# Prompt attention scores of a hybrid decoder step: from zero-padded keys, head by head, to 64-partition keys, heads in pairs

## The chip, the cores and the metric

The kernel runs on one core of a Trainium2 chip. The metric is the device time of one execution in microseconds (us). All data and all matmuls are float32. Five engines work beside each other: TensorE (PE, with its weight loads listed apart as PEld), VectorE (DVE), ScalarE (ACT), GpSimd (POOL) and SyncE (SP), which issues the transfers.

## The reference, cut to what matters

One layer takes 512 prompt tokens and 8 sequences of 4 new tokens over a paged cache. It has latent attention (MLA, 8 heads) and sparse attention (NSA, 8 heads in 2 groups of 4, each group with its own keys and values of 64 numbers). The change lies in NSA for the prompt. It has three branches; with 8 selected blocks at most, the selected branch sees all earlier tokens of a 512-token prompt, as the window branch does:

```python
s = einsum('btghd,bngd->bghtn', q, k_compressed) * 64**-0.5     # branch 1: 32 compressed blocks
p = masked_softmax(s, cmp_end[None, :] <= q_pos[:, None])
...
s = einsum('btghd,bkgd->bghtk', q_rot, k_sel_or_win) * 64**-0.5 # branches 2 and 3: rotated queries, causal
o = einsum('bghtk,bkgd->btghd', masked_softmax(s, causal), v)
out = gate0 * o_cmp + gate1 * o_sel + gate2 * o_win             # then * silu(z), one output projection, LayerNorm
```

## The kernel before, in words

`plan()` writes one list of steps by hand, and every engine walks this same list and issues its part of each step in that order; semaphores hold an engine back until what it needs is there. Stages follow each other: input projections and the compression of the caches (0 to about 290 us of the profile), then a stage in which the decode attention of the 8 sequences and the prompt's NSA are woven together (290 to 526), then the prompt's MLA with the output projections (526 to 675).

The prompt's attention is cut into units `UNITS`: a tile i of 128 queries, a branch (`pcmp`, `psel`, `pwin`, `pmla`) and a head h (for `pcmp` a group). NSA has 4 x (2 + 8 + 8) = 72 units, and `psel` and `pwin` 64 of them. A unit is a line of work over four engines: `scores` on TensorE into one of two PSUM banks (pool S); on VectorE a scaled and masked copy into a slot of `Pp` with the row minimum (`min_unit`), which frees the bank; on ScalarE the exponential (`exp_unit`); on TensorE i+1 transposes (`turn_p`) into one of two banks of pool T; a copy to `PTp` by ScalarE for even units and VectorE for odd ones; and on TensorE i+1 products with the values (`values`). `slot(m)` puts the scores of unit m, the transposes of unit m - `T_LAG` and the values of unit m - `V_LAG` into one step of the plan. `weave` then mixes the 72 slots with the decode steps by their weights, so that decode steps fill the gaps between slots. Pool T serves the decode steps too (transposes of key pages and of probabilities).

The queries of the two groups lie in the two halves of the partitions: `qrT` holds, for each hh, head hh of group 0 in partitions 0 to 63 and head hh of group 1 in 64 to 127. The keys `selKT` and `winKT` lie in the same way. Scores of one head are taken over all 128 partitions: GpSimd has made `padK` in the buffer `mid`, in which each group's keys stand in their half and the other half is zero (the steps `pad`). The compressed branch (`pcmp`) takes its scores over 64 partitions already, four small matmuls per group. A matmul of the program is two in the trace, each with its weight load, since its float32 weights are taken in two pieces; a transpose is one.

The lines that the steps below speak of: 828 and 833 projections, 803 every transpose (`turn`), 968, 969 and 971 scores of the decode items, 1021 their values, 1034 compressed scores, 1050 scores of `psel` and `pwin`, 1044 of `pmla`, 1081 values, 1669 and 1675 the masked copies, 1392 the exponentials, 1471 and 1817 the copies to `PTp`, 1911 and 1915 the padded keys.

## Time and profile before

| what | value |
|---|---|
| median of 3 runs | 674.38 us (672.66 to 680.26) |
| span of the profiled execution (from its first to its last instruction; no time of its own beside the span is recorded) | 675.0 us |
| busy: PE, DVE, ACT, POOL | 609.6, 286.9, 214.3, 93.7 us |
| mean granted clock of TensorE, 1 being 2.4 GHz | 0.960 |

Busy time is the union of an engine's instructions; matmuls are pipelined, so that a matmul's listed duration is longer than the distance to the next one's start. In this text the cost of a piece of TensorE's work is the distance between starts. A name such as `64*128` in a TensorE row is the size of the piece of the array that the instruction uses, rows by columns.

### The profile page before, as it was taken

The page shows a single profiled execution, that of the slowest core. Times are in us where ns is not written, and L with a number is a line of the kernel's source. Part 1 is how long each engine was busy: PE and PEld are TensorE (multiplying, and loading weights), DVE is VectorE, ACT ScalarE, POOL GpSimd, SP SyncE. Part 2 cuts the span into 40 slices and gives each one's busy share as a digit, 9 for nine tenths or more (in the row PEclk, how much of TensorE's full clock was granted, in tenths as well). Part 3 has the DMA queues.
Part 4 walks back from the last instruction along what each step waited for, and adds up shares of the span by engine and source line. Part 5 has one row for each costly group of instructions (what it writes and reads, how often), then busy time and mean ns, then how long its engine had stood idle before and what let it go on. Part 6 is the DMA issues. An engine that isn't in the chain of part 4 may idle for free. (4 is left out here: it accounts for less than half of the span.)

```text
span 675.0 us, 10193 instructions
## 1 busy us (share of the span) xinstructions
PE 609.6 (90%) x3482; PEld 375.2 (56%) x3482; DVE 286.9 (43%) x758; ACT 214.3 (32%) x614; POOL 93.7 (14%) x175
## 2 busy tenths in 40 slices
PE   6889998978897999879999899999999898999995
PEld 3554554555566865554446366666566765465642
DVE  0122202263658455653345334445444345255335
ACT  1330102241324221242343243445245345053310
POOL 0114531110100320420010001021003121000000
PEclk9889997989897989959999989999999998999999
DMA  8916563368407512223302105032401701010101
GB/s 307 263 47 144 106 155 51 47 87 118 100 1 236 212 26 74 74 74 110 109 18 70 57 1 188 1 111 79 125 2 62 289 2 40 1 62 1 63 0 62
DMA packets 42381, 60.34 MB, mean 89 GB/s; under 512 B 8986, under 2 KB 34074, under 8 KB 41722
## 3 DMA queue, kind: packets, MB, share of 16 engines
q1 hardware_dynamic: 42330, 59.69, 32.3%
q8 instruction: 28, 0.46, 0.3%
q14 instruction: 23, 0.19, 0.1%
HBM read 55.43 MB, written 8.41 MB: 95 GB/s over the span
## 5 line engine op out<-in xcount | busy, mean ns | idle before, releaser
L828 PE MATMUL psum<-wring,bufA 128*128 128x512 f32 (+2 forms) x384 | 159.2, 570 | 2.0 <-DMA wring<-in_w_in 2.0
L828 PEld LDWEIGHTS psum<-wring,bufA 128*128 128x128 f32 x384 | 74.9, 200 | 72.8 <-issue 67.4
L1392 ACT ACTIVATE wring<-wring,small 128x128 f32<-128x128 f32 (+3 forms) x96 | 53.9, 561 | 160.4 <-DVE small L1675 160.0
L1675 DVE CUSTOM_DVE_ANT_0 wring<-psum,const 128x128 f32<-128x128 f32 (+3 forms) x96 | 46.6, 486 | 86.5 <-PE psum L1050 75.1
L803 PE MATMUL psum<-const,ring 128*128 128x128 f32 (+2 forms) x360 | 52.2, 281 | 24.7 <-ACT mid L590 11.8
L803 PEld LDWEIGHTS psum<-const,ring 128*128 128x128 f32 (+2 forms) x360 | 37.9, 138 | 38.6 <-ACT mid L590 13.7
L1278 PE MATMUL psum<-ring,comp 128*128 128x512 f32 x128 | 56.5, 595 | 1.5 <-issue 1.5
L803 PE MATMUL psum<-const,wring 128*128 128x128 f32 x272 | 49.6, 280 | 6.8 <-ACT wring L1471 3.9
L803 PEld LDWEIGHTS psum<-const,wring 128*128 128x128 f32 x272 | 34.2, 143 | 33.6 <-issue 18.5
L1050 PE MATMUL psum<-mid,qrT 128*128 128x128 f32 (+3 forms) x128 | 50.1, 475 | 2.2 <-DVE small L1669 2.2
L1081 PE MATMUL psum<-kv,wring 128*128 128x64 f32 x320 | 43.8, 268 | 1.0 <-DVE rtmp L1703 0.8
L590 DVE COPY mid<-psum 64x256 f32<-64x256 f32 (+1 forms) x80 | 30.5, 381 | 32.6 <-PE psum L803 31.7
L1081 PEld LDWEIGHTS psum<-kv,wring 128*128 128x128 f32 x320 | 41.7, 195 | 3.0 <-DVE rtmp L1703 1.9
L1278 PEld LDWEIGHTS psum<-ring,comp 128*128 128x128 f32 x128 | 23.8, 190 | 29.0 <-issue 29.0
L891 PE MATMUL psum<-mid,w1h 128*128 128x256 f32 (+1 forms) x160 | 33.8, 366 | 0.0
L1954 POOL TENSOR_TENSOR bufA<-bufA,rtmp 128x512 f32<-128x512 f32 x8 | 10.2, 1271 | 151.4 <-DVE rtmp L1703 151.4
L891 PEld LDWEIGHTS psum<-mid,w1h 128*128 128x128 f32 x160 | 28.5, 197 | 4.1 <-issue 1.0
L590 ACT COPY mid<-psum 64x256 f32<-64x256 f32 (+1 forms) x80 | 26.7, 334 | 12.2 <-PE psum L803 11.0
L1050 PEld LDWEIGHTS psum<-mid,qrT 128*128 128x128 f32 x128 | 20.6, 200 | 16.6 <-issue 13.3
L1334 ACT COPY zsil<-psum 128x512 f32<-128x512 f32 (+1 forms) x16 | 6.7, 422 | 62.0 <-PE psum L828 58.9
L1843 DVE SCALAR_TENSOR_TENSOR bufA<-bufA,psum 128x512 f32<-128x512 f32 x8 | 5.5, 688 | 48.2 <-PE psum L1278 48.2
L1817 DVE COPY wring<-psum 128x128 f32<-128x128 f32 (+3 forms) x52 | 24.5, 471 | 2.7 <-PE psum L803 2.5
(227 smaller groups left out, 811.3 us busy)
## 6 DMA issues: line engine op xcount, KB each, us to landing
wring<-in_w_in SPq DMA_DIRECT2D x4, 2048.0 KB, 8.6
ring<-in_cache_cmp_kv SPq DMA_DIRECT2D x64, 128.0 KB
ring<-in_cache_mla SPq DMA_DIRECT2D x64, 80.0 KB, 1.9
ring<-in_cache_sel_kv SPq DMA_DIRECT2D x40, 128.0 KB, 2.1
ring<-in_state_win_kv SPq DMA_DIRECT2D x8, 512.0 KB, 5.4
ring<-in_w_o SPq DMA_DIRECT2D x1, 4096.0 KB, 13.7
out_s_win<-in_state_win_kv SPq DMA_DIRECT2D x1, 4064.0 KB
wring<-in_cache_sel_kv SPq DMA_DIRECT2D x24, 128.0 KB, 2.1
```

The costliest lines, as they stand in the source:

```text
L590: ins = copy(chT[z * HD:(z + 1) * HD, k, g, 2 * j:2 * j + 2, 0:n], bank[g * HD:(g + 1) * HD, :, z, :])
L803: return pe.transpose(out, in_, ident[0:in_.shape[0], 0:in_.shape[0]])
L828: ins = pe.matmul(bank[:, 0:w], xT[:, c, t * P:(t + 1) * P], wr[:, b % 2, c, 0:w], start=(c == 0), stop=(c == KC - 1))
L891: ins = pe.matmul(out, w1[:, k, c, :, :].rearrange("p r e -> p (r e)"), chT[:, k, :, c, 0:n], start=(c == 0), stop=(c == 7))
L1050: ins = pe.matmul(bank[:, 0:keys], qrT3[:, hh, q], padK[:, int(kind == "pwin"), g, 0:keys], start=True, stop=True)
L1081: ins = pe.matmul(bank[:, h * HD:(h + 1) * HD], PTp[:, n % 4, j * P:(j + 1) * P], v, start=(j == 0), stop=(j == i))
L1278: ins = pe.matmul(bank, mixT[:, n % 2, c, :], wo[:, c, half * 512:(half + 1) * 512], start=(c == 0), stop=(c == KC - 1))
L1334: act.copy(z[:, c0:c1], src)
L1392: ins = act.activation(Pp[:, n % 4, 0:w], Pp[:, n % 4, 0:w], ACT.Exp, bias=nmp[:, k, h:h + 1], scale=-1.0, accum_out=lp[:, k, h:h + 1])
L1675: ins = dve.tensor_tensor_reduce(Pp[:, n % 4, 0:w], bank[:, 0:w], mask, -(MLA_SCALE if kind == "pmla" else NSA_SCALE), CLAMP, ALU.add, ALU ...
L1817: dve.tensor_copy(PTp[:, n % 4, 0:w], arrive(T, u)[:, 0:w]).then_inc(T.free[u % T.n], 1)
L1954: pool.tensor_tensor(acc, acc, otmp, ALU.add).then_inc(summed, 1)
```

## The change

Four things change together. The scores of `psel` and `pwin` read `selKT` and `winKT` themselves, in the 64 partitions of the head's group; the steps `pad` and the semaphore `pad_ready` are gone, and the first such score waits for the copy of the last keys instead. The heads of a branch are taken in the order 0, 4, 1, 5, 2, 6, 3, 7, one of each group after the other. A slot of the plan now holds two units: two scores, then two units' transposes, then two units' values; the plan weaves 36 double slots with the same decode steps. The lags are 4 and 6 units in place of 3 and 5, and there are 8 probability slots; the four new ones (`Pq`) lie where `padK` was. Units of `pmla` keep their order, with the longer lags.

```diff
-UNITS = ([(i, kind, h) for i in range(PT) for kind in KINDS[:3] for h in range(G if kind == "pcmp" else H)]
+HEAD_ORDER = [g * HG + hh for hh in range(HG) for g in range(G)]
+UNITS = ([(i, kind, h) for i in range(PT) for kind in KINDS[:3] for h in (range(G) if kind == "pcmp" else HEAD_ORDER)]
...
-T_LAG, V_LAG = 3, 5
+T_LAG, V_LAG = 4, 6
+P_SLOTS = 8
...
-    cmp += [([("pad", 0)], .5), ([("pad", 1)], .5)]
...
+    def slot(m, width=1):
+        units = range(m, m + width)
+        now = [("pscore", n) for n in units if n < NU]
+        now += [("pturn", n - T_LAG) for n in units if T_LAG <= n < NU + T_LAG]
+        for n in units:
+            n -= V_LAG
+            if not 0 <= n < NU:
+                continue
+            now.append(("pvalue", n))
+            if n + 1 == NU or UNITS[n + 1][:2] != UNITS[n][:2]:
+                now.append(("branch", *UNITS[n][:2]))
         return now
...
-    p = [(slot(m), cost(m)) for m in range(N_NSA)]
+    p = [(slot(m, G), G * cost(m)) for m in range(0, N_NSA, G)]
...
-        padK = take(2 * G * SEQ).rearrange("p (b g n) -> p b g n", b=2, g=G)
+        Pq = take(2048).rearrange("p (s n) -> p s n", s=4)
...
+        def p_of(n):
+
+            k = n % P_SLOTS
+            return Pp[:, k, :] if k < 4 else Pq[:, k - 4, :]
...
-                    if h == 0 and i == 0:
-                        pe.wait_ge(pad_ready, 1 + int(kind == "pwin"))
+                    if kind == "psel" and h == 0 and i == 0:
+                        wait_copied(pe, T, T.at("post", B_WINGATE, NT - 1))
                     g, hh = h // HG, h % HG
-
-                    ins = pe.matmul(bank[:, 0:keys], qrT3[:, hh, q], padK[:, int(kind == "pwin"), g, 0:keys],
-                                    start=True, stop=True)
+                    s, kT = slice(g * HD, (g + 1) * HD), selKT if kind == "psel" else winKT
+
+                    ins = pe.matmul(bank[:, 0:keys], qrT3[s, hh, q], kT[s, 0:keys], start=True, stop=True)
...
-                if step[0] == "pad":
-
-                    j = step[1]
-                    wait_full(pool, B, B.at("hid", NT - 1, 0))
-                    ok(pool.memset(padK[:, j], 0.0))
-                    wait_copied(pool, T, T.at("post", B_WINGATE, NT - 1))
-                    for g in range(G):
-                        s = slice(g * HD, (g + 1) * HD)
-                        ins = pool.tensor_copy(padK[s, j, g, :], (selKT, winKT)[j][s, 0:SEQ])
-                    ins.then_inc(pad_ready, 1)
-                    pool.wait_ge(pad_ready, j + 1)
```

How the order on TensorE changes is seen in tile 2, at the end of `psel` and the start of `pwin`. Before (scores read `mid` and `qrT`, transposes `wring`, values `kv`; the rows on `ring` transpose key pages of a decode item, and `w1h` with `bufA` is a decode score):

```order
L1050 MATMUL psum<-mid,qrT 128x384
L803 MATMUL psum<-const,wring 128x128 x3
L1081 MATMUL psum<-kv,wring 128x64 x3
L971 MATMUL psum<-w1h,bufA 32x512 x2
L1050 MATMUL psum<-mid,qrT 128x384
L803 MATMUL psum<-const,wring 128x128 x3
L1081 MATMUL psum<-kv,wring 128x64 x3
L803 MATMUL psum<-const,ring 128x128 x4
L1050 MATMUL psum<-mid,qrT 128x384
L803 MATMUL psum<-const,wring 128x128 x3
L1081 MATMUL psum<-kv,wring 128x64 x3
L803 MATMUL psum<-const,ring 128x128 x4
```

The same place in the changed program, whose line numbers are five or six higher:

```order
L976 MATMUL psum<-w1h,bufA 32x512 x2
L1056 MATMUL psum<-selKT,qrT 128x384 x2
L808 MATMUL psum<-const,wring 128x128 x6
L1086 MATMUL psum<-kv,wring 128x64 x6
L808 MATMUL psum<-const,ring 128x128 x8
L1056 MATMUL psum<-winKT,qrT 128x384 x2
L808 MATMUL psum<-const,wring 128x128 x6
L1086 MATMUL psum<-kv,wring 128x64 x6
L976 MATMUL psum<-w1h,bufA 32x512
L808 MATMUL psum<-const,bufA 128x128 x8
```

Two scores stand next to each other, and decode steps that were parted by a unit now follow each other without one. Between the first and the last NSA score the decode work lies in 56 runs before and in 32 runs after; it is the same work. A score stands behind a matmul of another array size 24 times out of 64 before; in the changed program a pair of scores does so 30 times out of 32, and something of another size follows every pair.

The decode items' values show how TensorE's program lists matmuls that use different columns of the array (the program before, tile 2; `ring` and `wring` hold pages of different sequences, and each sequence has 32 columns of its own):

```order
L1021 MATMUL psum<-ring,w1h 32x128 x2
L1021 MATMUL psum<-wring,w1h 32x128 x2
L1021 MATMUL psum<-ring,w1h 32x128 x2
L1021 MATMUL psum<-wring,w1h 32x128 x2
L1021 MATMUL psum<-ring,w1h 32x128 x2
```

The changed program has these rows unmoved. On GpSimd the padded keys stood between two pairs of gate products:

```order
L1895 TENSOR_TENSOR zsil<-zsil,rtmp 128x512 x2
L1911 MEMSET mid 128x1024
L1915 COPY mid<-selKT 64x512 x2
L1911 MEMSET mid 128x1024
L1915 COPY mid<-winKT 64x512 x2
L1895 TENSOR_TENSOR zsil<-zsil,rtmp 128x512 x2
```

In the changed program the six rows are one, four gate products after each other.

## Rows read from the trace of the kernel before

**Rows 1.** Windows: busy us (and instructions) by engine, granted clock, DMA share, GB/s.
```profile
core 0: us, PE busy (x) PEld busy (x) DVE busy (x) ACT busy (x) POOL busy (x), PEclk, DMA share, GB/s
0.00:290.00 290.00, 257.84 (x1400) 158.00 (x1400) 117.26 (x216) 73.13 (x203) 60.42 (x129) 0.95 0.48 120
...
290.00:303.50 13.50, 10.87 (x36) 7.41 (x37) 5.70 (x28) 6.30 (x29) 2.48 (x6) 0.50 0.29 73
303.50:395.70 92.20, 83.44 (x492) 46.92 (x490) 39.30 (x163) 33.11 (x119) 6.34 (x5) 1.00 0.23 67
...
399.20:526.00 126.80, 122.73 (x883) 77.35 (x883) 57.04 (x184) 53.68 (x138) 14.59 (x19) 1.00 0.25 76
```

**Rows 2.** Waits of TensorE, 303 to 526 us: total us, times, longest.
```profile
PE psum L803 <- ACT wring L1471: 5.8, 11, 1.6
...
PE psum L803 <- DVE w1h L1635: 0.2, 1, 0.2
```

**Rows 3.** Source line 1050: all its matmuls, ns, first and last start, forms.
```profile
L1050 PE MATMUL psum<-mid,qrT x128: 275/486/954, 291.1 to 525.8; 128*128 128x128 f32 x32, 128*128 128x256 f32 x32, 128*128 128x384 f32 x32, 128*128 128x512 f32 x32
```

**Rows 4.** Timeline of PE, two units: start us, us, instruction, count.
```profile
313.12 0.39 PE L1050 MATMUL psum<-mid,qrT 128*128 128x128 f32 x2
313.34 0.27 PE L803 MATMUL psum<-const,wring 128*128 128x128 f32 x1
...
492.96 1.02 PE L1050 MATMUL psum<-mid,qrT 128*128 128x512 f32 x2
493.82 0.60 PE L803 MATMUL psum<-const,wring 128*128 128x128 f32 x4
```

**Rows 5.** Timeline of PE, a unit of 128x128 and a compressed unit behind it.
```profile
335.13 0.27 PE L803 MATMUL psum<-const,wring 128*128 128x128 f32 x1
335.24 0.33 PE L1081 MATMUL psum<-kv,wring 128*128 128x64 f32 x2
335.41 0.44 PE L1050 MATMUL psum<-mid,qrT 128*128 128x128 f32 x2
...
336.07 0.33 PE L1081 MATMUL psum<-kv,wring 128*128 128x64 f32 x2
336.34 1.08 PE L1034 MATMUL psum<-comp,qnT 64*128 64x32 f32 x8
337.34 0.33 PE L803 MATMUL psum<-const,wring 128*128 128x128 f32 x1
337.51 0.33 PE L1081 MATMUL psum<-kv,wring 128*128 128x64 f32 x2
```

**Rows 6.** Timeline of PE, a score behind decode values (128*32).
```profile
503.55 1.12 PE L1050 MATMUL psum<-mid,qrT 128*128 128x512 f32 x2
504.51 0.60 PE L803 MATMUL psum<-const,wring 128*128 128x128 f32 x4
```

**Rows 7.** Timeline of PE, the first two compressed units, next to each other.
```profile
286.78 1.55 PE L1034 MATMUL psum<-comp,qnT 64*128 64x32 f32 x16
288.26 0.63 PE L803 MATMUL psum<-const,wuk 128*64 128x128 f32 x4
```

**Rows 8.** Timeline of PE, decode values of four sequences, each in 32 columns.
```profile
436.53 0.30 PE L1021 MATMUL psum<-ring,w1h 128*32 128x128 f32 x2
436.54 0.30 PE L1021 MATMUL psum<-wring,w1h 128*32 128x128 f32 x2
436.66 0.28 PE L1021 MATMUL psum<-ring,w1h 128*32 128x128 f32 x2
```

**Rows 9.** Timeline of GpSimd: the first and the last padded keys.
```profile
272.09 0.95 POOL L1911 MEMSET mid<- 128x1024 f32 x1
...
275.44 1.43 POOL L1915 COPY mid<-winKT 64x512 f32<-64x512 f32 x2
```

**Rows 10.** Timeline of PE: the first score, and the last decode values; in brackets the wait.
```profile
291.06 0.79 PE L1050 MATMUL psum<-mid,qrT 128*128 128x128 f32 x2 [2.17 <-DVE small L1669]
...
523.83 0.48 PE L1011 MATMUL psum<-kv,w1h 32*128 32x128 f32 x2 [0.56 <-ACT w1h L1378]
```

More of the change, by code:

```diff
@@ L258, in plan @@
          for now, w in s for n in [turn_parts(*now[0]) if now else 0] for part in range(max(n, 1))]
-    def slot(m):
-        now = []
-        if m < NU:
-            now.append(("pscore", m))
-        if T_LAG <= m < NU + T_LAG:
-            now.append(("pturn", m - T_LAG))
-        if V_LAG <= m < NU + V_LAG:
-            now.append(("pvalue", m - V_LAG))
-        n = m - V_LAG
-        if 0 <= n < NU and (n + 1 == NU or UNITS[n + 1][:2] != UNITS[n][:2]):
-            now.append(("branch", *UNITS[n][:2]))
+    def slot(m, width=1):
[9 more added lines that the diff above has]
+                now.append(("branch", *UNITS[n][:2]))
         return now
@@ L276, in cost @@
         return 0.5 if kind == "pcmp" else 0.4 * (i + 1) + 0.2
-    p = [(slot(m), cost(m)) for m in range(N_NSA)]
+    p = [(slot(m, G), G * cost(m)) for m in range(0, N_NSA, G)]
     for t in range(PT):
-        p.insert(N_NSA // 2 + 18 + 4 * t, ([("vup", t)], .6))
-    p.insert(N_NSA, ([("qup", 0)], 1))
+        p.insert(N_NSA // 4 + 9 + 2 * t, ([("vup", t)], .6))
+    p.insert(N_NSA // G, ([("qup", 0)], 1))
     p.append(([("qh", 0)], 1))
@@ L557, in build @@
         bd_ready = sem("bd_ready")
-        pad_ready = sem("pad_ready")
         sp_min, sp_exp, sp_norm = sem("sp_min"), sem("sp_exp"), sem("sp_norm")
@@ L1059, in turn_p @@
                 for j in range(1 if kind == "pcmp" else i + 1):
-                    ins = turn(bank[:, j * P:(j + 1) * P], Pp[:, n % 4, j * P:(j + 1) * P])
+                    ins = turn(bank[:, j * P:(j + 1) * P], p_of(n)[:, j * P:(j + 1) * P])
                 ins.then_inc(T.full[u % T.n], 1)
@@ L1387, in exp_unit @@
                         c, s = h * HG + hh, slice(hh * CHP, (hh + 1) * CHP)
-                        ins = act.activation(Pp[:, n % 4, s], Pp[:, n % 4, s], ACT.Exp, bias=nmp[:, k, c:c + 1],
+                        ins = act.activation(p_of(n)[:, s], p_of(n)[:, s], ACT.Exp, bias=nmp[:, k, c:c + 1],
                                              scale=-1.0, accum_out=lp[:, k, c:c + 1])
@@ L1391, in exp_unit @@
                     w = (i + 1) * P
-                    ins = act.activation(Pp[:, n % 4, 0:w], Pp[:, n % 4, 0:w], ACT.Exp, bias=nmp[:, k, h:h + 1],
+                    ins = act.activation(p_of(n)[:, 0:w], p_of(n)[:, 0:w], ACT.Exp, bias=nmp[:, k, h:h + 1],
                                          scale=-1.0, accum_out=lp[:, k, h:h + 1])
@@ L1668, in min_unit @@
                         c = h * HG + hh
-                        ins = dve.tensor_tensor_reduce(Pp[:, n % 4, s], bank[:, s],
+                        ins = dve.tensor_tensor_reduce(p_of(n)[:, s], bank[:, s],
                                                        C("cmpmask")[:, i * CHP:(i + 1) * CHP], -NSA_SCALE, CLAMP,
@@ L1674, in min_unit @@
                     mask = const[:, a_tri - i * P:a_tri + P]
-                    ins = dve.tensor_tensor_reduce(Pp[:, n % 4, 0:w], bank[:, 0:w], mask,
+                    ins = dve.tensor_tensor_reduce(p_of(n)[:, 0:w], bank[:, 0:w], mask,
                                                    -(MLA_SCALE if kind == "pmla" else NSA_SCALE), CLAMP,
```

## The prediction

> **What bounds the kernel now.** I read the windows first. In the stage that mixes decode steps with the prompt's sparse attention, TensorE is busy 83.4 of 92.2 us and 122.7 of 126.8 us, while VectorE and ScalarE stay under half, GpSimd and the transfers lower still [rows 1]. So the time of this stage is TensorE's own work, and what shortens that work shortens the kernel until a wait takes its place. The waits of TensorE come next: nine kinds of them, 12.3 us in the 222 us from 303 to 526, the largest a transpose that waits for ScalarE to empty a bank, 5.8 us in 11 pieces, at most 1.6 us [rows 2]. No transfer is among them. The stage begins at the lower clock level, 1.2 GHz (granted 0.50 from 290 to 303.5), and runs at 2.4 GHz (1.00) in the two long stretches after that [rows 1]. The time of a matmul I take from the timeline, as the distance between starts.
>
> **Overlap of the two scores: the gain.** The 64 scores are 128 matmuls in the trace, 32 of each of four widths [rows 3]. A score whose weight load is hidden costs 0.22 us at 128 columns (313.12 to 313.34) and 0.86 us at 512 (492.96 to 493.82) [rows 4]. The widths between lie on the line between these ends: 0.43 and 0.65. Taking only 64 partitions makes none of them shorter: the columns that stream through stay the same. What can be won is that the two heads of a pair use different rows of the array and stream together. The trace has that for rows: two compressed units, next to each other and on different halves of the partitions, take 1.48 us (286.78 to 288.26) [rows 7], one alone 1.00 (336.34 to 337.34) [rows 5]. One after the other they would take 2 x 1.00 less one change of the array's size (0.2, below), 1.8 us, so loads and matmuls of the two halves did run together in part, the second unit ending 0.48 us after the first alone would. For long streams the trace has it for columns: four sequences' values begin within 0.02 us of each other, and the next two pieces 0.13 us after the first [rows 8]. If a pair costs one score, each of 8 pairs per tile saves one: 8 x (0.22 + 0.43 + 0.65 + 0.86) = **17.3 us**.
>
> **Change of the array's size: a cost.** Pairs use 64*128, their neighbours 128*128 or 128*32. Entering: values to a score of the same size take 0.17 us (335.24 to 335.41), the same values to the 64*128 unit 0.27 (336.07 to 336.34), so 0.10 us until the array is empty [rows 5]; and the first weight load is then not hidden, a score behind 128*32 work taking 0.96 us (503.55 to 504.51) [rows 6] against 0.86 [rows 4], 0.10 more. Together 0.20. Leaving: no row shows the emptying apart, so I take 0.10 for it as at the entry; and the transpose behind it takes 0.17 us (337.34 to 337.51) where one behind a score of its own size takes 0.11 (335.13 to 335.24) [rows 5], 0.06 more. Together 0.16. In the changed order 30 pairs enter from another size and all 32 leave to one: 30 x 0.20 + 32 x 0.16 = 11.1 us. Before, 24 scores behind a matmul of another size paid the entry: 4.8 us. Net **+6.3 us**.
>
> **Compressed units.** Three more pairs of groups come to stand next to each other (the first pair does already): before 2 x (1.00 + 0.10 + 0.06) = 2.32 us, then 1.48 + 0.16 = 1.64 [rows 5, 7]. 3 x 0.68 = **-2.0 us**.
>
> **Padded keys.** GpSimd's memsets and copies end at 276.9 us (275.44 + 1.43) [rows 9], the first score starts at 291.06 [rows 10]. They cost nothing now and their removal gives nothing; what hides them is 14 us of projections. The wait that replaces them is for the copy from which these same copies read, so it is long met, and nothing queues behind it. The plan weaves the compression with two steps less, which shifts a projection past a few transposes or products at half a dozen places from about 190 us on; all is the same work, and TensorE idles 32 us in the 290 us before the stage [rows 1]. I put this at 0, between -1.6 and +1.6, the longest single wait of the stage [rows 2].
>
> **Head and tail of the stage.** The first score now waits 2.17 us until VectorE has emptied one bank [rows 10]; the pair waits for both. At least 0, at most that wait again; I take +0.5, since the second bank's reductions follow on at once. At the end, three decode steps that depend on each other (probabilities, values, their transposes) stand without a prompt unit between them. One such wait is 0.56 us now [rows 10]; between 0 and 3 x 0.56 = 1.7, I take +0.8.
>
> **Lags, slots, waits inside the stage.** Two scores go out together, VectorE does two reductions in a row, ScalarE two exponentials, and only then comes ScalarE's copy of the even unit's transposes. With four or five scores between a unit's scores and its transposes (three before) the transposes should find their exponentials done, while decode transposes right behind a double slot wait longer for that copy. The 12.3 us of waits [rows 2] could go to nothing or double; I take 0 for their change, between -6 and +12, as the first effect takes some and the second gives some. The longer lag of the MLA units has the same work at its end, one slot later: 0. The eight probability slots cost no instruction. Without them a score of a double slot would overwrite a slot whose transposes stand later in the same double slot.
>
> **The sum.** -17.3 + 6.3 - 2.0 + 0 + 0.5 + 0.8 + 0 = -11.7 us. The profiled execution has 675.0 us, so 663.3; the median of the runs shown, 674.38, lies 0.6 below, which gives **663 us**.
>
> **Rival 1: starts in program order.** Each score is two matmuls, and if no matmul may start before an earlier one has, the second head's first piece starts with the first head's second piece. A pair then costs three halves of a score, half of the 17.3 comes back: 663 + 8.6 = 672. For it speaks that the trace has no long streams on different rows. Against it, four sequences' first pieces begin before the first sequence's second piece does [rows 8], though the program lists two matmuls of one buffer and then two of the other, each of two pieces. The Trainium skill, TensorE: Matmul & The Clock Gate, section on packing small matmuls, states this rule: matmuls start and end strictly in program order, and only weight loads overtake. Row 436.54 of the trace disagrees, unless pieces of different matmuls are interleaved in the instruction stream.
>
> **Rival 2: no overlap at all,** the change doing on the chip nothing but turn the array's size: 663 + 17.3 = 680. Rows 7 speak against it.
>
> **Rival 3: the gain goes back into waits.** TensorE's work per double slot falls, and the others' does not; at tile 0, where a score is 0.22 us and an exponential with its copy is longer, transposes and decode steps wait for ScalarE. Some 7 us, more than half of today's waits [rows 2] once more: 670. Against it, VectorE and ScalarE are under half busy [rows 1]. The Trainium skill, TensorEngine Tiling, section PSUM Bottleneck, warns that tiling speeds TensorE but not the emptying of PSUM, which may become the bound; by rows 1 it would not.
>
> **Rival 4, slower: the decode chain shows.** The same decode work lies in 32 runs between prompt units where it lay in 56. Inside a run transposes, copies, scores and probabilities wait for each other through two banks, and a prompt unit no longer covers the copy. The price is at most the longest wait of today, 1.6 us [rows 2], per run. At half of it 32 x 0.8 = 26 us more, 689. It makes the kernel slower from 11.7 / 32 = 0.37 us per run, and by over 1% from 0.6. Against it, 12.3 us over the 56 runs of today are 0.22 each, and a longer run also has work of other items in it.
>
> **How the numbers follow.** Overlap with the waits about as they are: 0.64 (of this 0.05 below 654). Rival 1: 0.10. Rival 2: 0.05. Rival 3: 0.12. Rival 4: 0.09. The likeliest gives 663. Range 654 to 676: below, the waits fall by 6 and the weave gives its 1.6; above, rivals 1 and 3 are in, and rivals 2 and 4 and the 0.05 are left out. A measurement of this kernel tells about 1% from no change, which is 667.6 and 681.1. Faster: the forecast and a little of rival 3, 0.67. Same: rivals 1, 2 and most of 3, with rival 4's mild end, 0.25. Slower: 0.08.
>
> **What would show it.** In the changed profile the second score's matmuls must begin within about 0.02 us of the first's, and the distance from a pair's start to the next transpose must be about 0.96 + 0.10 us at 512 columns (rival 1: 1.5, rival 2: 1.9). Behind a pair the first transpose must take 0.06 more. TensorE's waits in the stage must stay near 12 us; at 20 rival 3 holds, at 30 rival 4. The forecast is wrong as well if the clock falls to 1.2 GHz for long inside the stage, or if the first 13.5 us of it [rows 1] no longer run at that level.

## The result, and the profile after

The changed kernel takes **699.98 us** (median of 4 runs, 692.75 to 703.67) where the kernel before takes 673.52; the ratio is 1.034 (95% interval 1.024 to 1.044). It is slower, and the forecast of 663 us was wrong in size and in sign. Single runs of one kernel differ by up to 4%, with the clock that they were granted, so the ratios here leave out those over 1.5% above its fastest, and two of the kernels below have no ratio.

The stages first. Of before, the stage that mixes decode steps with the sparse prompt attention starts with the first compressed score at 286.8 us, the MLA scores start at 530.6, the end is at 675.0: 286.8, 243.8 and 144.4 us. Of after the same points lie at 280.9, 544.9 and 697.4: 280.9, **264.0** and **152.5** us. So the time ahead of the stage gained 6 us, the mixed stage lost 20 and the MLA stage 8.

The windows of the changed kernel, with the columns of [rows 1]: the time ahead of the stage, its four query tiles, the MLA stage, one stretch inside the first tile, and the 5 us ahead of that stretch.

```profile
0.00:280.90 280.90, 249.38 (x1380) 153.66 (x1380) 113.62 (x213) 71.47 (x197) 55.12 (x122) 0.96 0.50 124
280.90:341.10 60.20, 53.43 (x196) 25.63 (x194) 22.57 (x82) 17.12 (x69) 5.96 (x8) 0.69 0.29 84
341.10:399.00 57.90, 51.87 (x325) 29.47 (x324) 23.89 (x99) 22.49 (x78) 3.80 (x3) 0.93 0.13 38
399.00:460.70 61.70, 56.96 (x436) 37.32 (x435) 27.91 (x98) 24.02 (x75) 6.09 (x7) 0.93 0.24 76
460.70:544.90 84.20, 78.38 (x501) 47.87 (x502) 36.49 (x115) 33.24 (x84) 8.52 (x12) 0.92 0.21 66
544.90:697.40 152.50, 131.45 (x648) 83.96 (x648) 64.66 (x154) 44.98 (x113) 9.85 (x17) 0.96 0.14 53
284.80:318.90 34.10, 31.25 (x82) 13.96 (x82) 9.47 (x41) 9.35 (x40) 3.15 (x6) 0.50 0.34 97
279.80:284.80 5.00, 3.22 (x56) 2.67 (x44) 4.94 (x7) 2.11 (x8) 1.55 (x2) 1.00 0.31 81
```

The column to read is the granted clock, third from the end. In [rows 1] it is 0.50 for 13.5 us at the stage's start and 1.00 in the two long stretches after that. Here it falls after 5 us in which TensorE is busy for 3.22, stays at 0.50 for 34.1 us, although TensorE is busy in 31.25 of them, and it is below 1.00 in every tile. A stretch of d us at a mean of c holds 2 x (1 - c) x d us at 1.2 GHz; over the four tiles that is some 68 us, where the same four tiles of before have 17.

Next the matmuls of a pair. The timeline of PE in the changed kernel, with the columns of [rows 4], shows a pair of 512 columns that overlaps, one that does not, and a pair of 128 columns.

```profile
517.22 1.13 PE L1056 MATMUL psum<-winKT,qrT 64*128 64x512 f32 x4
518.28 0.98 PE L808 MATMUL psum<-const,mid 128*128 128x128 f32 x7
...
525.03 1.12 PE L1227 MATMUL psum<-ckvT,wuk 128*128 128x512 f32 x2
526.09 1.12 PE L1056 MATMUL psum<-winKT,qrT 64*128 64x512 f32 x2
527.42 1.12 PE L1056 MATMUL psum<-winKT,qrT 64*128 64x512 f32 x2 [0.21 <-ACT wring L1461]
528.48 0.77 PE L808 MATMUL psum<-const,wring 128*128 128x128 f32 x5
...
321.86 0.49 PE L1056 MATMUL psum<-winKT,qrT 64*128 64x128 f32 x4
322.29 0.33 PE L808 MATMUL psum<-const,mid 128*128 128x128 f32 x1
```

Where a pair overlaps, its second score begins 0.01 us after the first, and the next transpose follows 1.06 us after the start at 512 columns (517.22 to 518.28) and 0.43 at 128: the 0.96 + 0.10 that the prediction asked for. But only 21 of the 32 pairs do that. At 526.09 the second score begins 1.33 us late. Ahead of the pair stands a key product (line 1227) that holds one of the two score banks, and the second score waits until ScalarE has copied it (line 1461). Four of the eight widest pairs go that way.

TensorE's waits in the changed kernel, with the columns of [rows 2], 303 to 540 us, the five largest groups:

```profile
PE psum L808 <- ACT wring L1476: 10.4, 12, 2.1
PE psum L808 <- ACT w1h L1371: 2.4, 7, 0.6
PE psum L808 <- ACT w1h L1383: 1.3, 4, 0.3
PE psum L808 <- DVE w1h L1628: 1.3, 2, 1.0
PE psum L1039 <- DVE mid L1812: 0.7, 1, 0.7
```

All groups together are 17.4 us where [rows 2] had 12.3. The compressed pair, last, behaves as its row of before did [rows 7]: 1.48 us to the transpose behind it, now in later tiles too, where the clock is 1.00.

```profile
341.10 1.55 PE L1039 MATMUL psum<-comp,qnT 64*128 64x32 f32 x16
342.58 0.49 PE L808 MATMUL psum<-const,mid 128*128 128x128 f32 x2
```

So the overlap is there, the waits are 5 us more, and most of the loss seems to be clock. Three theories were set against each other. **A**: scores on 64 partitions, or their overlap, lower TensorE's clock. **B**: the longer runs of decode steps between double slots do it. **C**: the longer lags cost the MLA stage its 8 us.

### The profile page after: what moved, and what is told of

The parts are those of the page before. It is cut to its first block and busy times, and to the rows that moved or that the text cites. A ratio compares the mean times of both kernels' runs of the same rounds, so it can differ in the third digit from the quotient of the medians.

```text
span 697.4 us, 10182 instructions
## 1 busy us (share of the span) xinstructions
PE 621.5 (89%) x3482; PEld 377.9 (54%) x3482; DVE 289.1 (41%) x758; ACT 213.3 (31%) x614; POOL 89.3 (13%) x169
## 5 line engine op out<-in xcount | busy, mean ns | idle before, releaser
L808 PE MATMUL psum<-const,ring 128*128 128x128 f32 (+2 forms) x360 | 56.5, 304 | 24.4 <-ACT mid L590 11.2
L808 PEld LDWEIGHTS psum<-const,ring 128*128 128x128 f32 (+2 forms) x360 | 41.2, 146 | 40.1 <-issue 13.8
L1397 ACT ACTIVATE mid<-mid,small 128x128 f32<-128x128 f32 (+3 forms) x48 | 26.8, 558 | 78.3 <-DVE small L1680 78.1
L1397 ACT ACTIVATE wring<-wring,small 128x128 f32<-128x128 f32 (+3 forms) x48 | 26.7, 556 | 68.9 <-DVE small L1680 68.8
L808 PE MATMUL psum<-const,mid 128*128 128x128 f32 (+2 forms) x176 | 30.7, 296 | 11.7 <-DMA mid<-in_x_prompt 7.0
L808 PEld LDWEIGHTS psum<-const,mid 128*128 128x128 f32 (+2 forms) x176 | 21.5, 151 | 29.7 <-issue 22.8
L1680 DVE CUSTOM_DVE_ANT_0 wring<-psum,const 128x128 f32<-128x128 f32 (+3 forms) x48 | 22.3, 486 | 35.4 <-PE psum L1056 25.0
L1948 POOL TENSOR_TENSOR bufA<-bufA,rtmp 128x512 f32<-128x512 f32 x8 | 10.2, 1271 | 178.0 <-DVE rtmp L1708 178.0
L1680 DVE CUSTOM_DVE_ANT_0 mid<-psum,const 128x128 f32<-128x128 f32 (+3 forms) x48 | 22.4, 486 | 21.4 <-PE psum L1056 19.8
L1049 PE MATMUL psum<-wring,ring 96*128 96x128 f32 (+3 forms) x64 | 26.0, 489 | 5.2 <-DVE small L1680 4.9
L808 PE MATMUL psum<-const,wring 128*128 128x128 f32 x148 | 25.7, 298 | 3.5 <-ACT wring L1476 2.4
```

The costliest lines, as they stand in the source:

```text
L808: return pe.transpose(out, in_, ident[0:in_.shape[0], 0:in_.shape[0]])
L1049: ins = pe.matmul(bank[:, 0:keys], QT[:, i % 2, h, :], KT[:, h, 0:keys], start=True, stop=True)
L1397: ins = act.activation(p_of(n)[:, 0:w], p_of(n)[:, 0:w], ACT.Exp, bias=nmp[:, k, h:h + 1], scale=-1.0, accum_out=lp[:, k, h:h + 1])
L1680: ins = dve.tensor_tensor_reduce(p_of(n)[:, 0:w], bank[:, 0:w], mask, -(MLA_SCALE if kind == "pmla" else NSA_SCALE), CLAMP, ALU.add, ALU.m ...
```

## The experiments

Beside the ratio of each kernel to the kernel before, the tables give the mean granted clock of the same runs (0.962 for the kernel before), and the product of span and that clock, in us (646.6 before). The product is an estimate of what the span would be with all of it at 2.4 GHz: it rises with work and waits, and falls a little where half-clock time is time in which TensorE waits anyway.

**64 partitions alone.** The first kernel has the order, lags and single units of before, with scores over 64 partitions and no padded keys. Its edit against the changed kernel, cut:

```diff
-HEAD_ORDER = [g * HG + hh for hh in range(HG) for g in range(G)]
+HEAD_ORDER = list(range(H))
...
-T_LAG, V_LAG = 4, 6
+T_LAG, V_LAG = 3, 5
...
-    p = [(slot(m, G), G * cost(m)) for m in range(0, N_NSA, G)]
+    p = [(slot(m), cost(m)) for m in range(N_NSA)]
```

> The order of the kernel before (single units, natural head order, lags 3 and 5), with one edit alone: scores over 64 partitions and no padded keys. Nothing overlaps, every prompt unit has two changes of array size. Theory A in the form that 64-partition scores themselves lower the clock: half-clock time of the NSA stage 40 us or more instead of 17, time 690 to 700. Theory A in the form that only the overlap lowers it: half-clock time 15 to 25, time 674 + 6 to 10 for the size changes = 680 to 684. Theory B (long runs): as the second, 680 to 684. Theory C: the MLA stage is back at 144 to 146 us.

Its four runs took 686.85 to 714.66 us at clocks of 0.953 to 0.888; no run is under the slowest of before (684.11). Too spread for a ratio, so the edit was made smaller. The next kernel is the kernel before, padded keys and all, where a score reads the half of the partitions that is not zero:

```diff
-ins = pe.matmul(bank[:, 0:keys], qrT3[:, hh, q], padK[:, int(kind == "pwin"), g, 0:keys], ...)
+s = slice(g * HD, (g + 1) * HD)
+ins = pe.matmul(bank[:, 0:keys], qrT3[s, hh, q], padK[s, int(kind == "pwin"), g, 0:keys], ...)
```

> The kernel before in everything, its padded keys and its order included, but each selected and window score reads only the 64 partitions that hold its group (same result). One difference: 64 partitions instead of 128 in these scores. Measured in single units with 64 partitions, a score takes 0.09 us longer at 128 to 384 columns and 0.19 at 512, so 16 x (3 x 0.09 + 0.19) = 7 us more work. Theory A (scores on 64 partitions lower the clock): mean clock 0.92 to 0.94, time 690 to 702. Theory D (the clock was lost by what else differed, the missing pads and the moved start of the stage): mean clock 0.955 to 0.965 as before, time 679 to 683.

And the complement, the kernel before without pads and with 128 partitions. Its scores sum the keys of both groups, so that it does the same work and does not compute the reference:

```diff
-ins = pe.matmul(bank[:, 0:keys], qrT3[s, hh, q], kT[s, 0:keys], ...)   # from the first kernel above
+ins = pe.matmul(bank[:, 0:keys], qrT3[:, hh, q], kT[:, 0:keys], ...)
```

> The kernel before without the pad copies: lags 3 and 5, single units, scores over all 128 partitions of the unpadded keys (the two groups' keys are summed, so the values of the two branches are not the reference's). The run with the longer lags differs from this one by the lags and slots alone. Theory D (missing pads and moved start lower the clock): mean clock 0.93 to 0.945, 683 to 693. Theory A: 0.955 to 0.965, 672 to 676. Theory C (longer lags cost): this one is under the 695 of the run with lags 4 and 6 by 8 us or more, with the MLA stage at 143 to 146.

| kernel | ratio (95%) | clock | span x clock |
|---|---|---|---|
| before64 | 1.033 (1.026 to 1.039) | 0.942 | 654.0 |
| nopad128 | 0.993 (0.989 to 0.997) | 0.966 | 645.1 |

Theory A in its 64-partition form holds: the one edit costs 3.3%, some 22 us, where its product rises by 7. The windows of before64 (the four tiles, then two stretches near the border of the second and the third), and under them those of nopad128 (the four tiles, together 243.6 us where before has 243.8, the MLA stage, and two stretches near the same border):

```profile
283.90:334.70 50.80, 45.87 (x200) 23.77 (x198) 22.11 (x82) 17.50 (x70) 5.95 (x8) 0.87 0.34 100
334.70:394.20 59.50, 55.64 (x328) 31.04 (x327) 24.32 (x99) 22.86 (x78) 3.81 (x3) 0.96 0.12 36
394.20:461.90 67.70, 65.89 (x439) 40.17 (x438) 27.45 (x98) 24.80 (x75) 6.08 (x7) 0.91 0.24 73
461.90:548.70 86.80, 84.23 (x505) 49.82 (x505) 35.59 (x115) 33.79 (x84) 8.51 (x12) 0.92 0.22 70
384.10:389.10 5.00, 2.96 (x19) 1.99 (x20) 3.24 (x11) 1.34 (x4) 1.28 (x1) 1.00 0.00 0
389.10:406.10 17.00, 17.00 (x61) 12.34 (x60) 5.11 (x28) 6.82 (x27) 0.00 (x0) 0.50 0.00 0
```

```profile
279.60:329.00 49.40, 42.97 (x199) 23.48 (x197) 21.72 (x81) 17.07 (x68) 5.95 (x8) 0.86 0.35 102
329.00:385.50 56.50, 50.44 (x328) 30.00 (x327) 24.06 (x101) 22.93 (x80) 3.80 (x3) 1.00 0.13 38
385.50:446.60 61.10, 58.88 (x441) 38.62 (x439) 27.18 (x98) 24.80 (x75) 6.08 (x7) 0.97 0.26 79
446.60:523.20 76.60, 73.61 (x504) 46.72 (x505) 35.30 (x113) 33.76 (x84) 8.52 (x12) 1.00 0.25 80
523.20:667.70 144.50, 127.83 (x637) 80.46 (x636) 64.48 (x154) 44.31 (x112) 9.83 (x17) 0.98 0.14 51
383.20:388.20 5.00, 3.93 (x33) 3.42 (x31) 2.30 (x14) 3.16 (x13) 0.00 (x0) 1.00 0.00 0
388.20:391.60 3.40, 3.40 (x14) 2.63 (x14) 1.14 (x10) 1.94 (x12) 0.00 (x0) 0.51 0.00 0
```

In before64 TensorE is busy for 65.89 of 67.70 us in the third tile, more than in nopad128 (58.88 of 61.10), and the clock is lower (0.91 against 0.97). That does not clear idle time: the low stretch began at 389.1 us, ahead of the tile, after 5 us in which TensorE was busy for 2.96. In nopad128 the clock falls near the same border, after 3.93 busy us, and it is back after 3.4 us where before64 takes 17.0, all of them busy.

**Which part of it.** Two kernels add a matmul of 32 columns ahead of each padded score of the kernel before, into columns that the score then overwrites, once over 64 partitions (the array changes size on the way in and out) and once over 128 (no change is added). Counted in the traces, the stage has 141 changes of size in the kernel before and in the second of these, and 231 in the first: 90 more, since 36 of the 64 scores of before stand behind another size already. A third issues each 64-partition score of before64 twice.

```diff
+pe.matmul(bank[:, 0:32], qrT3[s, hh, q], padK[s, int(kind == "pwin"), g, 0:32], ...)   # before_switch
+pe.matmul(bank[:, 0:32], qrT3[:, hh, q], padK[:, int(kind == "pwin"), g, 0:32], ...)   # before_small128
+for _ in range(2):                                                                     # before64_twice
+    ins = pe.matmul(bank[:, 0:keys], qrT3[s, hh, q], padK[s, int(kind == "pwin"), g, 0:keys], ...)
```

> The kernel before, with one small matmul (64 partitions, 32 columns, into the bank that the score then overwrites) ahead of each selected and window score over 128 partitions: two changes of array size for each of 64 scores, as with scores on 64 partitions, and all the full-size work kept. It adds some 64 x 0.25 = 16 us. If the changes of size lower the clock: mean clock 0.92 to 0.945, 700 us or more. If it is the half-filled array during the scores: mean clock 0.955 to 0.965, 685 to 692.

> The kernel before with a small matmul (128 partitions, 32 columns, into the bank that the score then overwrites) ahead of each selected and window score: as the run with 64 partitions there, but the array never changes size. If the changes of size cost the clock: mean clock 0.955 to 0.965 and 680 to 690. If the small matmul itself does (a stretch in which the array loads weights and streams few columns): mean clock 0.93 to 0.94 and 700 or more.

> The kernel before with each selected and window score read from the 64 partitions of its group and issued twice. Against the run with single ones it adds 16 x (0.21 + 0.32 + 0.42 + 0.53) = 24 us at full clock. If 64-partition work counts as half and any work helps: mean clock back at 0.95 to 0.965, 697 to 712. If work on 64 partitions lowers the clock the more of it there is: mean clock 0.92 to 0.94, 715 to 735.

| kernel | ratio (95%) | clock | span x clock |
|---|---|---|---|
| before_switch | 1.061 (1.055 to 1.067) | 0.934 | 666.3 |
| before_small128 | 1.018 (1.010 to 1.027) | 0.955 | 656.1 |
| before64_twice | 1.068 (1.061 to 1.075) | 0.958 | 687.9 |

The two small matmuls differ in nothing but the rows that they use. They did not run beside each other; the kernel before, run beside each, had clocks of 0.962 and 0.957. The windows of the mixed stage, of the 5 us ahead of the low stretch at the second tile's end, and of that stretch, before_switch and then before_small128:

```profile
286.60:565.10 278.50, 265.59 (x1596) 166.48 (x1595) 109.36 (x392) 98.84 (x306) 24.34 (x30) 0.91 0.22 66
397.00:402.00 5.00, 3.08 (x23) 2.40 (x21) 3.63 (x14) 1.69 (x6) 1.27 (x1) 1.00 0.00 0
402.00:422.50 20.50, 20.50 (x74) 15.73 (x73) 5.90 (x29) 7.08 (x28) 0.00 (x0) 0.50 0.00 1
```

```profile
283.40:540.00 256.60, 242.84 (x1596) 156.56 (x1595) 108.80 (x393) 98.84 (x306) 24.33 (x30) 0.95 0.24 72
384.40:389.40 5.00, 2.82 (x22) 2.25 (x21) 3.17 (x13) 1.91 (x6) 1.27 (x1) 1.00 0.00 0
389.40:396.20 6.80, 6.80 (x29) 5.90 (x28) 2.21 (x7) 3.20 (x8) 0.00 (x0) 0.50 0.01 2
```

With all the full-size work of before in place, 90 more changes of size cost 10.2 us of the product (666.3 - 656.1, an estimate of 0.11 each) and 0.021 of the clock, together 4%. The low stretch lasts 20.5 us in place of 6.8 (and 3.4 more a little later); the 5 us ahead of it are about alike, 3.08 and 2.82 us busy. So the changes of size, with the small matmul that makes them, lower the granted clock while every score keeps 128 partitions. Whether streaming on half the partitions adds to that stays open: before64_twice, with twice as much of it between the same changes, took 719 to 720 us at 0.958 in three runs, and 738 and 740 us at 0.926 in two. The Trainium skill, TensorEngine Tiling (Array Packing), Key Properties, says that a change of tiling mode drains TensorE. The estimate of 0.11 us per change agrees with it. Why a low stretch lasts longer with such changes no run here shows.

**More work into the changed kernel.** One more matmul ahead of each pair's first score, over 128 or over 64 partitions:

```diff
+if g == 0:
+    pe.matmul(bank[:, 0:keys], qrT3[:, hh, q], kT[:, 0:keys], start=True, stop=True)   # extra128
+    pe.matmul(bank[:, 0:keys], qrT3[s, hh, q], kT[s, 0:keys], start=True, stop=True)   # twice64
```

> The changed kernel with one more matmul in front of each pair of selected or window scores: same columns, all 128 partitions, into the bank that the pair's first score then overwrites. It adds 8 x (0.22 + 0.43 + 0.65 + 0.86) = 17 us of TensorE work at full clock, and no wait. Theory A (the kind of work counts): half-clock time of the NSA stage falls from 68 us to 20 to 45, and the time is 699 + 17 - 12 to 24 = 692 to 704. Theory B (idle stretches and long runs of decode steps count, which stand as they were): half-clock time 55 to 75, 712 to 718.

> As the run with one more matmul over 128 partitions, but the one added reads 64 partitions (the first score of each pair is issued twice): the same 17 us of added time, the same place. Theory A (the kind of work counts, and 64 partitions count less): half-clock time of the NSA stage stays at 55 us or more or grows, 712 to 720, well over the run with 128 partitions. If any added work helps, both runs have the same half-clock time within 12 us and their times are within 6 us.

They measured 1.046 (1.040 to 1.052) and 1.043 (1.038 to 1.048), at clocks of 0.942 and 0.943 against 0.931 of the changed kernel, with products of 661.0 and 659.8 against 647.5. Some 13 us of added work cost, by the ratios, 6 to 8 us of time; the intervals meet that of the changed kernel. The forms with 128 and with 64 partitions come out alike, which is against the expectation that the kind of work counts; the clock is higher by 0.011 or 0.012 in either.

**The order without 64 partitions.** The changed kernel's order, and single units with the longer lags, both with scores over all 128 partitions of the unpadded keys (the same line as in nopad128, and like it not the reference):

> The order of the changed kernel exactly (head pairs, double slots, lags 4 and 6, eight slots), but each selected and window score reads all 128 partitions of the unpadded keys, so that no two scores overlap and the array never changes size there. (The keys of both groups are summed in these scores, so the two branches' values are not the reference's.) Theory A, the clock falls because scores on 64 partitions, or their overlap, leave TensorE with less full-size work: the half-clock time of the NSA stage goes from 68 us back to 17 to 25, and the time is 675 to 687 (the overlap's 17 us are lost, some 6 of size changes and 22 to 26 of clock come back). Theory B, the clock falls because decode steps and units now stand in longer runs: half-clock time stays at 55 to 70 us and the time is about 700 + 17 - 6 = 711. Theory C, the longer lags cost the MLA stage 8 us: that stage stays at 150 to 153 us here as well.

> The order of the kernel before (single units, natural head order) with lags 4 and 6 and eight slots, and scores over all 128 partitions of the unpadded keys (keys of both groups summed, values of the two branches not the reference's): what is left of the change is the lags, the slots and the missing pad copies. Theory C: the MLA stage takes 150 to 153 us instead of 144.5 and the time is 678 to 683. Theories A and B: no clock lost, NSA stage 243 us, time within 1% of 674; the MLA stage then stays at 144 to 146.

pairs128 measured 1.019 (1.010 to 1.029) at 0.950, by three of its four runs. lags128, which differs from nopad128 by the lags alone, took 682.92 to 701.37 us in its four runs, where the twelve of nopad128 took 667.51 to 679.35; the two fastest, 682.92 and 690.44, have a clock of 0.954. The windows of lags128, the second tile and the MLA stage, and its largest waits in the latter:

```profile
329.10:391.70 62.60, 57.81 (x326) 33.07 (x325) 23.87 (x100) 21.73 (x78) 4.03 (x4) 0.86 0.13 37
534.00:688.60 154.60, 133.60 (x648) 86.00 (x648) 64.61 (x154) 45.05 (x113) 9.84 (x17) 0.94 0.13 46
```

```profile
PE psum L1049 <- DVE small L1680: 4.9, 3, 2.1
PE psum L808 <- ACT wring L1476: 4.9, 5, 1.5
```

nopad128 takes 144.50 us there, with these waits:

```profile
PE psum L808 <- ACT wring L1476: 3.8, 5, 2.1
PE psum L1049 <- DVE small L1680: 1.8, 2, 1.0
```

Theory C holds: with the longer lags alone, the MLA scores wait 4.9 us for VectorE's reductions instead of 1.8, and the stage is 10 us longer, some 6 us of it clock by the two windows (0.94 against 0.98). All six profiles with lags 4 and 6 have an MLA stage of 152.5 to 159.7 us, the thirteen others one of 142.7 to 150.4; some of those are low in clock too. Why the reductions come later is not shown. The mixed stage of lags128 is also 10 us longer than that of nopad128 (254.0 against 243.6 us): its second tile runs at 0.86, where nopad128 has 1.00. So in this one profile the lags cost clock without a single 64-partition score of these branches. The missing pads, which with the eight slots are all that sets nopad128 apart from before, are worth 0.7%; it lies ahead of the stage, which begins at 279.6 us, while tiles and MLA stage have the lengths of before.

**What the overlap is worth.** The changed kernel with heads in natural order, so that both scores of a pair use the same partitions and nothing can overlap, and the same for a kernel of the next part:

```diff
-HEAD_ORDER = [g * HG + hh for hh in range(HG) for g in range(G)]
+HEAD_ORDER = list(range(H))
```

> The changed kernel with the heads in their natural order, so that the two scores of a pair are of one group and read the same 64 partitions: double slots, longer lags and 64-partition scores stay, the overlap of selected and window scores alone is undone. If the overlap does what the two timelines show, this is slower than the changed kernel by up to 17 us at the same clock: 710 to 717. Theory A, overlap form: the clock comes back (half-clock time 20 to 30 instead of 68) and the time is 685 to 695. Theory A, 64-partition form, and theory B: clock as low as after, 705 to 717.

> The kernel with fine pairs (two scores pulled together, all else in single units, lags 3 and 5) with the heads in natural order, so that both scores of a pair read the same 64 partitions and nothing overlaps. If the overlap saves what the starts of the matmuls show in 21 of 32 pairs, some 12 to 15 us of work: span x clock 651 to 654 us instead of 639. If the clock depends on 64 partitions and not on the overlap: mean clock 0.935 to 0.945, time 692 to 700. If the overlap lowered the clock: 0.955 to 0.965, 678 to 684.

pairs_one_group: 1.041 (1.032 to 1.050) at 0.932; the changed kernel has 1.034 at 0.931. fine_one_group: 1.029 (1.019 to 1.038) at 0.936, by two of its four runs, its pairs with overlap 1.011 at 0.941. So the overlap takes off 0.7% (the intervals meet) and 1.8%, and it is not what lowers the clock. The product fell by less than expected in the second pair (646.6 to 638.9, where 651 to 654 was asked); the distances between starts of its score matmuls, at the granted clock, fell by 13 us.

**Lags and slots with pairs.** First the changed kernel with lags 3 and 5. Then pairs in tiles 2 and 3 only, tiles 0 and 1 as before:

```diff
-T_LAG, V_LAG = 4, 6                                    # lags35, and late_pairs too
+T_LAG, V_LAG = 3, 5
...
+p = [(slot(m), cost(m)) for m in range(single)]        # late_pairs; single: the first unit of tile 2
+p += [(slot(m, G), G * cost(m)) for m in range(single, N_NSA, G)]
```

> The changed kernel with the lags of the kernel before, 3 and 5, and nothing else undone. Theory C, now put as: the longer lags cost score waits in the MLA stage (4.9 us in 3 instead of 1.8 in 2) and with them some clock: the MLA stage goes from 152.5 back to 144 to 146 us and the time to 686 to 692. Theory A, the scores on 64 partitions lower the clock of the NSA stage: its half-clock time stays at 45 us or more, so that the time does not go below 684. Rival, the lags are the whole loss: half-clock time of the NSA stage 17 to 25, time 665 to 676. Rival, double slots need the longer lags: transposes wait for the exponentials of the pair, waits of the NSA stage rise from 23 us to 28 or more, time 697 or more.

> Tiles 0 and 1 as before (padded keys of 256 columns, scores over 128 partitions, single units), tiles 2 and 3 in pairs over 64 partitions, lags 3 and 5 everywhere, six slots. Of the overlap 8 x (0.65 + 0.86) = 12 us remain, of the size changes about 3, so 674 - 9 = 665 at the clock of before. Theory A in the form that what counts is the stretch at the stage's start, where decode work on few rows alternates with short scores: mean clock 0.95 to 0.967 as before, 660 to 670. Theory A in the form that scores on 64 partitions lower the clock wherever they stand: half-clock time appears in tiles 2 and 3 (before 3.4 us), mean clock 0.93 to 0.945, 676 to 688.

lags35: 1.018 (1.012 to 1.024) at 0.950 by three runs of 683 to 691 us; its three others took 699 to 705 us, one of them the profiled run, where the waits from 297 to 550 us are 23.6 us. So it is not clear of the changed kernel (693 to 704 us). late_pairs: 1.020 (1.014 to 1.025) at 0.954. The windows of late_pairs and its largest waits from 397 to 534 us:

```profile
284.40:333.90 49.50, 43.09 (x199) 23.46 (x198) 21.75 (x82) 17.11 (x69) 5.95 (x8) 0.86 0.34 100
333.90:390.40 56.50, 50.43 (x328) 29.96 (x327) 24.01 (x101) 22.88 (x80) 3.81 (x3) 1.00 0.15 43
390.40:451.60 61.20, 53.69 (x440) 34.18 (x439) 26.70 (x98) 24.07 (x75) 6.08 (x7) 1.00 0.25 77
451.60:533.90 82.30, 74.86 (x504) 44.89 (x505) 36.17 (x114) 33.32 (x84) 8.50 (x12) 0.98 0.21 65
```

```profile
PE psum L1096 <- DVE bufA L1718: 3.0, 2, 1.6
PE psum L1084 <- DVE rtmp L1718: 3.0, 2, 1.6
PE psum L1096 <- DVE rtmp L1718: 2.9, 2, 1.4
```

Tiles 0 and 1 are those of nopad128 to 0.1 us. In tile 2 TensorE works 5 us less (53.69 against 58.88) and the tile is no shorter: the products with the values wait for VectorE to empty their bank, which the kernel before shows once, with 0.8 us. Double slots with the short lags have a new wait, and with the long ones another.

So the next two kernels pull only the two scores together and leave transposes and values in single units, with lags 3 and 5, in all tiles and in tiles 2 and 3:

```diff
+def slot(m, first=0):
+    now = [("pscore", n) for n in ((m, m + 1) if first == 1 else () if first == 2 else (m,)) if n < NU]
+    if T_LAG <= m < NU + T_LAG:
+        now.append(("pturn", m - T_LAG))
...
+p = [(slot(m, 1 + m % 2), cost(m)) for m in range(N_NSA)]        # fine_pairs; fine_late: from tile 2 on
```

> Pairs over 64 partitions in all tiles as in the changed kernel, but only the two scores are pulled together: turns and values stay in single units between the decode steps, with lags 3 and 5. If the waits came from double slots and longer lags: waits of the NSA stage 15 to 20 us instead of 23 (29.6 with double slots and lags 3 and 5), MLA stage 143 to 146 at full clock. Work 10 to 15 us under before. Theory A (pairs on 64 partitions lower the clock): mean clock 0.92 to 0.94, 675 to 690. Theory B (double slots and long runs of decode steps lowered the clock): mean clock 0.955 to 0.965, 655 to 663.

> Tiles 0 and 1 as before with padded keys, in tiles 2 and 3 the pairs of scores pulled together, everything else in single units, lags 3 and 5, six slots. Late pairs in double slots kept the clock of before (0.954) and lost their gain to 9 us of waits, 685 us. If those waits came from the double slots, NSA waits go from 27 us back to 17 to 20 and the time is 668 to 675. If the waits come with the pairs themselves, 680 to 687.

The last kernel is fine_late with kup and cscore steps that stand right ahead of a pair put behind it (`woven` is the list of steps):

```diff
+for n in range(single, N_NSA, 2):
+    at = woven.index(("pscore", n))
+    for j in range(at - 1, at - 5, -1):
...
+        if woven[j][0] in ("kup", "cscore"):
+            step = woven.pop(j)
+            at = woven.index(("pscore", n + 1))
+            while woven[at][0] != "pvalue":
+                at += 1
+            woven.insert(at + 1, step)
...
```

> The kernel with fine pairs in tiles 2 and 3 only, with two steps kup and cscore that stood right ahead of a pair put behind the unit that follows it. There the pair's second score started 0.42, 1.04 and 1.33 us after the first instead of 0.01, because both score banks were not free. If that is the cause, these pairs now start within 0.01 us, 2.8 us of work go, and the time is 669 to 673, at most 1% under before. If not, the starts stay as they were and the time is 674.

| kernel | ratio (95%) | clock | span x clock |
|---|---|---|---|
| fine_pairs | 1.011 (1.007 to 1.014) | 0.941 | 638.9 |
| fine_late | 0.998 (0.995 to 1.002) | 0.957 | 642.5 |
| fine_late_moved | 0.994 (0.991 to 0.997) | 0.961 | 641.7 |

fine_pairs has the lowest product of all and still loses to before, by the clock alone; theory B gets nothing from it, since turns and values stand between the decode steps as before and the clock is as low as in before64. fine_late_moved is the fastest of the kernels that compute all of the reference, 669.45 us against 675.17 of the kernel before, run beside it. All its 16 pairs overlap; the pair that waited behind a product, and the last two tiles:

```profile
508.30 1.13 PE L1077 MATMUL psum<-winKT,qrT 64*128 64x512 f32 x4
509.36 0.66 PE L825 MATMUL psum<-const,mid 128*128 128x128 f32 x4
```

```profile
391.20:448.20 57.00, 53.52 (x439) 33.64 (x438) 26.98 (x98) 24.64 (x76) 6.08 (x7) 1.00 0.28 84
448.20:523.00 74.80, 69.16 (x505) 43.11 (x505) 34.72 (x115) 33.13 (x84) 8.52 (x12) 1.00 0.24 74
```

Both tiles keep 1.00 and are 4 and 2 us shorter than in nopad128.

## Why the prediction was wrong

**The step that failed first is the change of the array's size.** The prediction booked it as 6.3 us of time and held the clock as it was; it named a falling clock at the end, as something that would overturn the forecast, and gave it no price and no chance. In time the prices were near: a pair of 512 columns takes 1.06 us to the transpose behind it where a score took 0.86, the 0.10 + 0.10 that were asked; why the product gives less, 0.11 per change, is not worked out. The count was off: 36 scores of before, not 24, stand behind another size, since transposes of 32 or 64 columns are such too, so that by the same prices the net is 11.1 - 7.2 = 3.9 us. In clock it costs more than in time: with 64 partitions and nothing else changed 0.962 becomes 0.942, and the time 3.3% more. In the profiled runs the mixed stage went from 17 to 68 us at 1.2 GHz; if half of the added 51 us is lost, that is 25 us, more than the 20 by which the stage grew. In the same stage before64 and fine_pairs, with the short lags, have 44 us at 1.2 GHz, and lags128, without the added size changes, has 34. So of the added 51 us the size changes bring the larger part, some 27, and the longer lags some 17, as far as one profile of each can tell.

**Lags, slots, waits: taken as 0. This step failed too.** The bounds of -6 to +12 held the measured +5.1 us of waits in the stage (17.4 - 12.3). But "the same work at its end, one slot later: 0" for the MLA units was wrong: the longer lags alone cost that stage 10 us in lags128, in waits for VectorE and in the clock that goes with them. As steps of the ratio: single units without pads 0.993, fine pairs on 64 partitions 1.011, double slots 1.018, longer lags 1.034. The shares depend on the order in which the steps are taken: by way of the longer lags first, nopad128 0.993, lags128 some 1.02, pairs128 1.019, and then 64 partitions with their overlap 1.034, the lags cost more than the size changes.

**Overlap of the two scores: right in kind, mis-sized.** The second score starts 0.01 us behind the first, and rival 1's rule, starts in program order, would have needed half a score (0.53 us at 512 columns). But 17.3 us supposed that all 32 pairs overlap, and 21 did, worth 11.3 us by the prediction's prices. A pair needs both score banks at once, and key, value and compressed products that use the same two banks stood right ahead of most of the others. The prediction did not ask which banks such products hold. Summed at the granted clock and without waits, the scores went from 39.1 to 30.2 us, 8.9 less, with the part of the size changes that falls on them; no single row holds these sums. The Trainium skill, TensorEngine Tiling (Array Packing), Gotcha 1: PSUM Pressure, warns that row tiling asks more of the PSUM banks. The runs agree: with the products moved away all 16 pairs of fine_late_moved overlap.

**Compressed units** came out as worked out (1.48 us to the transpose at full clock). **Padded keys** were not quite free: nopad128 gains 0.7%. **Head and tail of the stage**: the first score waits 2.17 us as before [rows 10] and its partner begins 0.44 us later, where +0.5 was taken; the decode values' wait is 0.5 us once, as in [rows 10], where +0.8 was.

**The rivals.** Rival 2 (no overlap) and rival 1 are out. Rival 3 came in part: transposes wait 10.4 us for ScalarE's copy where it was 5.8, and its mark of 20 us was not reached (17.4). In late_pairs the gain of tile 2 goes back into waits whole, but these are for VectorE and in a late tile, not for ScalarE in tile 0. Rival 4 forecast slower, 689, for a reason that the runs do not bear out: the waits on the decode items' own copies (`w1h`) are 5.5 us where they were 4.5, and fine_pairs, with the runs of decode steps of before, has the low clock too. That its time lay nearest to the measured one is luck.

## What to carry to other kernels

Where TensorE bounds a stage, price an edit by the granted clock as well as by its work: a change that swaps full-array work for smaller pieces between changes of array size can lose more clock than it saves in work. Here pairs in tiles 2 and 3 alone kept it (fine_late_moved, 1.00 in both), while pairs in all tiles (fine_pairs, mean 0.941) and single 64-partition scores (before64, 0.91 and 0.92 in these two tiles) lost it; why is not shown, so try such an edit tile by tile. Row-packed pairs want both their banks free at the same moment; look at what else uses that pool just ahead of them. Pull together only the instructions that overlap, and leave lags and slots as they are until a run has shown what each costs alone.

## What the runs showed that was not expected

- The clock stayed low while TensorE was busy: 0.50 over 34.1 us with 31.25 us of work in the changed kernel, and over 17.0 us with 17.0 in before64. It had fallen after 5 us with 3.22 and 2.96 us of work; a like fall in nopad128, after 3.93, lasted 3.4 us.
- Added work can be half paid back by the clock: 13 us of it, by the product, made the changed kernel only some 1% slower (1.034 to 1.046 and 1.043, with intervals that meet).
